# GpSimd's high part of each weight chunk: product with a constant for product with a tile of ones, loops unrolled

## What is computed

```python
def first_block(x, mem, ...):
    h = rms_norm(x, pre_norm_g)
    a_u, a_v, sq, sk, sv, mq, z = split(h @ w_in)          # 1024 x 2816
    mk, mv = split(rms_norm(mem, mem_norm_g) @ w_mem_kv)   # 1024 x 512
    ...
    return x + rms_norm(y @ w_out, post_norm_g)            # 1024 x 1024

def second_block(x, ...):
    h = rmsnorm(x, attn_norm)
    q, k, v, iq, ik, iw, z, xbc, dt_raw, gate_a, gate_b = split(h @ w_in)   # 1024 x 9320
    ...
    merged = sigmoid(gate_a) * (y_attn @ w_attn_branch) + sigmoid(gate_b) * (y_ssd @ w_ssd_branch)
    x = x + merged @ w_out
    return x + hier_moe(rmsnorm(x, ffn_norm), ...)
```

## Time and profile before

| | |
|---|---|
| device time, median of 3 runs | 1577.42 us (1576.61 to 1577.51) |
| profiled execution: device time | 1578.34 us |
| profiled execution: span of the core | 1576.5 us |
| granted TensorE clock, mean | 0.941 of 2.4 GHz |
| instructions in the trace | 18167 |

### The profile page before, as it was taken

One profiled execution on the slowest core, in us unless ns is written; L12 is line 12 of the kernel. 1 busy time (PEld: TensorE's weight loads), 2 busy tenths in 40 slices (PEclk: granted clock), 3 DMA queues, 4 the chain that ended last, 5 costly groups with the idle time before them and its releaser, 6 DMA issues.

```text
span 1576.5 us, 18167 instructions
## 1 busy us (share of the span) xinstructions
PE 1368.4 (87%) x7076; PEld 984.2 (62%) x7076; DVE 635.3 (40%) x929; ACT 378.2 (24%) x736; POOL 827.3 (52%) x712
## 2 busy tenths in 40 slices
PE   5898969589987978999999999968998499999993
PEld 5777747477766745678777878857877333333331
DVE  3131252324887056364877556463221411111112
ACT  3211053311130156311122544251003011111111
POOL 7678713537677710288888333749690213333320
PEclk9999989799999989999999999979997599999997
DMA  5423210132122210023222211352255079999964
GB/s 191 136 67 107 67 41 28 38 107 94 67 81 98 90 53 2 14 94 133 80 87 71 71 41 68 128 232 80 80 220 207 13 314 376 372 373 376 368 246 177
DMA packets 85237, 216.29 MB, mean 137 GB/s; under 512 B 23509, under 2 KB 32421, under 8 KB 71589
## 3 DMA queue, kind: packets, MB, share of 16 engines
q1 hardware_dynamic: 62076, 199.22, 33.7%
q0 software_dynamic: 13824, 8.44, 1.8%
q10 hardware_dynamic: 9256, 7.51, 1.5%
HBM read 255.99 MB, written 26.22 MB: 179 GB/s over the span
## 4 chain that ended last, share of the span: by engine, by line
PE 44%; issue 11%; POOL 11%; PEld 10%; DVE 9%; DMA 4%; DVEq 3%; ACT 3%; POOLq 3%; PEldq 2%; ACTq 1%; SPq 0%
PE ps L963 9%; PE ps L133 6%; PE ps L134 6%; PE ps L135 6%; POOL w_lo L487 6%; PE ps L975 5%; POOL w_hi L484 5%; PEld ps L133 4%; PEld ps L134 3%; PEld ps L135 3%; POOLq L485 2%; PE ps L734 2%; PE ps L955 2%; PE ps L822 1%; DMA w_gu<-w_up,over_u 1%
## 5 line engine op out<-in xcount | busy, mean ns | idle before, releaser
L484 POOL TENSOR_TENSOR w_hi<-stage,unit 128x512 fp32r<-128x512 f32 (+2 forms) x304 | 323.8, 1096 | 444.0 <-PE ps L135 434.3
L487 POOL TENSOR_TENSOR w_lo<-stage,w_hi 128x512 fp32r<-128x512 f32 (+2 forms) x304 | 404.7, 1362 | 10.8
L133 PE MATMUL ps<-hi,w_hi 128*128 128x512 f32 (+1 forms) x600 | 240.3, 401 | 31.8 <-POOL w_lo L487 17.9
L134 PE MATMUL ps<-hi,w_lo 128*128 128x512 f32 (+1 forms) x600 | 237.0, 395 | 0.0
L135 PE MATMUL ps<-lo,w_hi 128*128 128x512 f32 (+1 forms) x600 | 236.8, 395 | 0.0
L133 PE MATMUL ps<-w_hi,hi 128*128 128x512 f32 (+3 forms) x560 | 199.2, 356 | 12.6 <-POOL w_lo L487 6.6
L134 PE MATMUL ps<-w_hi,lo 128*128 128x512 f32 (+3 forms) x560 | 197.0, 352 | 0.0
L135 PE MATMUL ps<-w_lo,hi 128*128 128x512 f32 (+3 forms) x560 | 196.9, 352 | 0.0
L963 PE MATMUL ps<-w_gu,xT 128*64 128x512 f32 x768 | 172.0, 600 | 3.2 <-DMA w_gu<-w_up,over_u 1.8
L133 PEld LDWEIGHTS ps<-hi,w_hi 128*128 128x128 f32 x600 | 116.5, 194 | 63.1 <-issue 19.3
L135 PEld LDWEIGHTS ps<-lo,w_hi 128*128 128x128 f32 x600 | 116.4, 194 | 24.0
(11 more groups left out here) (393 smaller groups left out, 1714.7 us busy)
## 6 DMA issues: line engine op xcount, KB each, us to landing
stage<-w_in SPq DMA_DIRECT2D x84, 512.0 KB, 4.2
w_gu<-w_gate SPq DMA_DIRECT2D x32, 1024.0 KB, 11.6
w_gu<-w_up SPq DMA_DIRECT2D x32, 1024.0 KB, 13.7
w_dn<-w_down SPq DMA_DIRECT2D x32, 1024.0 KB, 12.0
stage<-w_out SPq DMA_DIRECT2D x16, 512.0 KB, 4.2
stage<-w_ssd_branch SPq DMA_DIRECT2D x16, 512.0 KB, 4.5
stage<-w_in SPq DMA_DIRECT2D x20, 256.0 KB, 3.0
stage<-w_attn_branch SPq DMA_DIRECT2D x8, 512.0 KB, 4.1
```

What stands on the lines that cost most here:

```text
L133: pe.matmul(out, x[0], w[0], start=first, stop=False)
L134: pe.matmul(out, x[1], w[0], start=False, stop=False)
L484: nc.gpsimd.tensor_tensor(w_hi[:, b, k, 0:n], stage[:, b, k, 0:n], unit[:].broadcast_to([P, n]), ALU.mult)
L487: last = nc.gpsimd.tensor_tensor(w_lo[:, b, k, 0:n], stage[:, b, k, 0:n], w_hi[:, b, k, 0:n].bitcast(F32), ALU.subtract)
```

## The change

The high part becomes a TENSOR_SCALAR with the constant 1.0, which has one input, in place of a TENSOR_TENSOR with a tile of ones; the tile, its memset and the drain behind it go. GpSimd's five loops and the narrow jobs between them become one loop of the text, so that all 37 jobs after the first stand one after another in its program, with the same waits, now against constants.

```diff
-        unit = sb("unit", [P, 1])
...
                 for k in range(HALF):
-                    nc.gpsimd.tensor_tensor(w_hi[:, b, k, 0:n], stage[:, b, k, 0:n], unit[:].broadcast_to([P, n]), ALU.mult)
+                    nc.gpsimd.tensor_scalar(w_hi[:, b, k, 0:n], stage[:, b, k, 0:n], 1.0, None, ALU.mult)
                 pool.drain()
...
-            nc.gpsimd.memset(unit[:], 1.0)
-            pool.drain()
             for b in range(2):
                 pool.wait_ge(w_in_sem[b], 32)
                 split(b, 512)
-            with pool.Fori(1, JOB_MQ) as i:
-                split_job(i)
-            split_job(JOB_MQ, 256)
-            with pool.Fori(JOB_MQ + 1, JOB_SMALL) as i:
-                split_job(i)
-            split_job(JOB_SMALL, SMALL)
-            with pool.Fori(JOB_SMALL + 1, JOB_Z) as i:
-                split_job(i)
-            with pool.Fori(JOB_Z, JOB_Z + 4) as i:
-                split_job(i, 256)
-            with pool.Fori(JOB_Z + 4, JOBS) as i:
-                split_job(i)
+            narrow = {JOB_MQ: 256, JOB_SMALL: SMALL, **{JOB_Z + i: 256 for i in range(4)}}
+            for i in range(1, JOBS):
+                split_job(i, narrow.get(i, 512))
```

## The result

The changed kernel takes 1595.16 us in the median (4 runs, 1592.45 to 1599.47), the kernel before 1577.01 us beside it: a ratio of 1.012, 95% interval 1.009 to 1.015. It is slower by 18 us, where 11.6 us of gain were forecast; the range 1560 to 1600 holds it, on the side of the first rival. The profiled execution took 1599.47 us, with a span of 1597.7 us, 21.2 us more than before.

The account below looks back on a forecast made before the run. TensorE, busy 87% of the span, was taken to bound the kernel, with GpSimd late at ten waits (26.4 us). Savings of 11.6 us from 1578.3 gave 1566.7, stated as 1566 us by the median; range 1560 to 1600.

Parts of the forecast that it names:

- the first rival: GpSimd's high part: one-input product no faster than the subtraction, 1.26 us each; +11 us, 1588.5; chance 37%, 9 for over 1.44 us.
- Where GpSimd matters: Only where TensorE waits for GpSimd's low parts: 26.4 us in 10 waits, nearly all a faster split can give back.
- the price of the new high part: One 128x512 one-input product on GpSimd: 0.70 us in place of 1.01, saving 1.24 us per wide split.
- those steps: GpSimd's memset time per column, 0.83 ns; the old product was read as two of them, one per input.
- the upper bound: Highest price allowed for the new 128x512 product on GpSimd, taken from the subtraction's row: 1.26 us.
- The list of places: TensorE's ten waits for low parts, each priced by the splits since GpSimd last waited; together 11.6 us saved.
- the start: Second chunk, 30.34 us: two splits back to back from the first DMA; 2.2 us saved, or 2 us lost if slower.
- the two waits beside short chunks: At 141.49 and 355.16 us, one wide split each beside a short chunk: 1.24 us saved each, 2.5 together.
- 498.82: TensorE's longest wait for low parts, 8.16 us, where VectorE's product catches the fourth high part; 1.6 us saved.
- the slot of 1.6: At the longest wait, one of eight GpSimd instructions less to fit between VectorE's: about 1.6 us saved.
- The unrolled program: GpSimd's loops written out: loop turns and instruction fetch both priced at 0; some 5 us if fetches stall at bad places.
- The steep part: Beyond 1.44 us per product a wide split exceeds TensorE's 10.95 us; at 2.0 us, +100 us; chance 9%.

Follow-up runs that it names:

- the long pieces: The unrolled kernel with high part (as TENSOR_COPY) and subtraction each one instruction of 128x4x512 in place of four: 1562.83 us, 0.990 of the kernel before.
- the copy's kernel: The changed kernel with a TENSOR_COPY in place of the TENSOR_SCALAR for the high part, in four pieces: 1552.2 us, 0.983 of the kernel before.

## Why the prediction was wrong

- *Where GpSimd matters* was right in the main: its longer splits reach the end through TensorE's waits for the low parts. They grew by 20.6 us, of which some 6 came back in other waits. The measured time lies in the range only through the first rival, on the other side of no change than the forecast.
- **The step that failed** is the price of the new high part: "The product is exactly two of those steps per column, as if its two inputs took turns. One input less then leaves one", and from it "I take 0.70 us". It is 1.465 us, three steps. It even lies above the upper bound, the subtraction's 1.26: another form's row didn't bound it. The reasoning from inputs fits the copy (0.57 us against the 0.58 worked out) and there alone; the product's two steps were no count of inputs either, since with a full tile as its second input it takes 2.6. The 0.25 us that the prediction gave to the subtraction's operation belong to its full second tile: with ones in its place the subtraction takes 1.01 us as well. The first rival named this case, "no faster than the subtraction", from 1.01 us on, at 37%. Why the scalar form takes three steps no run shows.
- The Trainium skill's rule that a form with one input runs at roughly line rate ("GPSIMD Engine Reference", Engine selection), which would have given 0.58 us, holds in these runs for the copy and not for the scalar product. The same page of the Trainium skill (Elementwise side-by-side cycle accounting) gives 2.6 cycles per element as the floor of two inputs: taking the memset's 0.83 ns per column as a cycle, that fits the subtraction and the product with a full tile, and not either of them with the broadcast column, which take two.
- *The list of places*, at the measured price, was good: 1.82 us more per wide split gives 3.6 us at the start (the second job began 4.1 us later), 1.3 and 2.3 us more at the two waits beside short chunks where 1.8 each was due. What it lacks at this price are the short new waits of 0.4 to 1.6 us, most of them at wide chunks: the prediction put their start at 1.44 us, and 1.465 is just past it.
- *498.82*: priced at 2 us for a slower product; the wait grew from 8.16 to 9.25. With the copy it shrank to 6.74, by 1.4 us, near the slot of 1.6, but not by the way told. The prediction held VectorE's product at its old time and had the four high parts through before it. In the copy's kernel VectorE comes 5.6 us sooner and GpSimd 3.3, and the third and fourth copies are caught:

```profile
476.56 10.66 POOL L483 CAST w_hi<-stage 128x512 fp32r<-128x512 f32 x4 [6.82 <-PE ps L135]
```

```profile
477.15 4.86 DVE L1551 TENSOR_TENSOR qt<-qt,st 128x4096 f32<-128x4096 f32 x1
```

That the number came near is luck.

- *VectorE's own time* was left out of the sum. It was the smaller part of the story. The Trainium skill's rule ("SBUF — State Buffer", Who interferes with whom) that one excludes the other for a whole instruction fits the product, the subtraction and the long pieces here, and not the scalar form, beside which eight VectorE instructions passed in 4.8 us. A VectorE that is held up less is the likely source of the some 6 us that the change got back, and of the copy's 7 us above the waits for low parts that it saved, which is what TensorE's wait for `xtok` lost (13.8 to 6.4 us). This last step is argued from VectorE's busy time, that wait and the shorter convolution stretch; no run changed VectorE's delay alone.
- *The unrolled program* costs nothing that can be told (at most 0.3%): right. The steep part, +100 us at 2.0 us, measured +86 at 1.99.

## What to carry to other kernels

On GpSimd count the form of an instruction and of its operands, not the number of its inputs: try each candidate alone, a few in a row before the kernel's first wait, before pricing an edit by its neighbours' rows. Look at what else ran in that stretch, for VectorE's instructions lengthen GpSimd's rows. Rounding or copying a tile there is a copy's work (0.57 us for 128x512), not an arithmetic form's. And look at both sides of the split: its length against the consumer's chunk, where the cost turns steep, and the length of a single piece against what the other engine, here VectorE, has to wait for: subtractions in four pieces won over one though each costs its fixed 0.15 us, while for the short copy the number of pieces made no difference that can be told.

## What the runs showed of the hardware

- GpSimd, 128x512 float32: copy 0.57 us, product or subtraction with a broadcast column 1.01, product or subtraction with a full tile 1.23, scalar form 1.46; rounding changed nothing in the three where both were tried (copy, product with the column, scalar form).
- An instruction of VectorE with one SBUF input loses least beside the scalar form, though that is the longest: 0.60 us in place of 0.37, against 1.20 beside the product with the broadcast column and 0.71 beside the copy.
- A memset on GpSimd, which reads nothing, still slows VectorE's form with one SBUF input (0.70 us) and not the one with two.
